# Modulation in four lots of columns, most of each summed on VectorE and used at once by gate and up tile

## The chip, the cores and the metric

The kernel runs on one core of a Trainium2 chip: TensorE (PE) for matmuls, VectorE (DVE), ScalarE (ACT) and GpSimd (POOL) for work on elements, SyncE (SP), whose queue issues nearly all transfers, SBUF as working memory and eight banks of PSUM, into which TensorE writes. The metric is device time in microseconds, the median of the runs.

## The reference

Two stacks of layers over 512 tokens of width 1024, in float32. What matters here is the very start: the conditioning vector c gives shift, scale and gate of each sub-layer, and the first sub-layer is a gated feed-forward.

```python
c_act = jax.nn.silu(c)
mod = c_act @ ada_w[i] + ada_b[i]
sh1, sc1, g1, sh2, sc2, g2, sh3, sc3, g3 = jnp.split(mod, N_MOD, axis=-1)
h = modulate(rms_norm(x, ln_ffn1[i]), sh1, sc1)
x = x + 0.5 * g1[:, None, :] * swiglu(h, ffn1_wg[i], ffn1_wu[i], ffn1_wd[i])
```

The first matmul of the feed-forward needs sh1 and sc1, 2048 columns of ada_w[0], which are 8 MB of weights: 1024 x 2048 values of 4 bytes.

## The kernel before

Activations lie transposed, 8 blocks (kb) of 128 features by 512 tokens. Every weight tile has 8 blocks of 256 columns, 1 MB. SP loads it into a slot of w_raw, ScalarE casts it in two halves to w_hi_t (w_hi counts them), GpSimd subtracts that from the raw values to give w_lo_t (w_lo), and each product is three matmuls: high x high, high x low and low x high, 48 matmuls of 512 columns a tile (16 blocks and column halves by 3). The activations are split the same way, into h_hi and h_lo. Tiles alternate between two slots; in a feed-forward a gate tile (slot 0, banks 0 and 1) and an up tile (slot 1, banks 2 and 3) make a pair. After a pair ScalarE takes Silu of the gate banks, VectorE multiplies (v_done), ScalarE copies the high part (a_hi_s), VectorE makes the low part (a_lo_s). The next pair's gate waits for v_done, since it writes the banks again.

Engines have a written order of instructions each, and meet by semaphores. At the start (SP lines 699 to 720) c, the identity, the first 256 columns of ada_w, six of eight blocks of shift columns in four quarters (first_a), x, and the 1024 scale columns in four quarters (first_b) are loaded, then the first gate and up tile. TensorE sums the first 256 columns itself (L2094, 16 matmuls of one column), VectorE the other 1792 as rows (L1477 and L1480: accumulator + row block of weights x c), of which TensorE adds up the partitions by matmuls with ones (first_sums, L2068). Then VectorE makes gain and mod of all 16 column blocks (ada_fin) and the normed input block by block: start_scaled (x * gain * root, L1525), ScalarE adds the shift into h_hi (L1101), start_low gives h_lo (L1531). The root of the mean square is in bank 6. start_units on TensorE (L2081 to L2085) follows with the gate tile alone; the up tile and all others run in unit (L1916 to L1921): all high products first, then the eight with w_lo.

While the feed-forward runs, VectorE also sums the next modulation columns: ada_step (L1427, L1430), one row block of 1024 columns each, out of a ring of four buffers that SP fills once mod_ok says that the first modulation is done; each eight steps end with a transpose and a reduce. Five steps go to each of the first four pairs, ahead of that pair's products on VectorE's queue. Between the first and the second pair stand two small matmuls for the attention bias (L2127, L2128).

## Time and profile before

| | us |
|---|---|
| median of 3 runs | 2597.61 (2597.54 to 2598.28) |
| the profiled execution | 2597.89 |
| its span | 2596.1 |
| TensorE busy in the span | 2555.4 |

The profiled execution is the one the rows below come from; its time is the span and what lies around it. Times in rows are counted from the start of the span. Busy times of an engine overlap those of the others, and a matmul's record is longer than the distance to the next, since matmuls are pipelined: the chain of waits shows the distance.

### The profile page before, as it was taken

What the parts mean: (1) busy time and instruction counts of PE and PEld (TensorE: products, weight loads), DVE (VectorE), ACT (ScalarE), POOL (GpSimd) and SP (SyncE); (2) the same over time, 40 slices, a digit from 0 to 9 for tenths busy, and PEclk for the clock granted to TensorE, in tenths of its full rate; (3) what the DMA queues carried; (4) which work ended last, traced back from release to release, by engine and by line L of the source; (5) the groups of instructions that cost most, each with busy time, mean ns of one, the idle gap of its engine ahead of it and who ended that gap; (6) DMA issues with size and microseconds to landing.
All of it is one profiled execution on the core that took longest, in us unless ns stands there. A gap on an engine that the chain in (4) does not pass through costs nothing.

```text
span 2596.1 us, 30205 instructions
## 1 busy us (share of the span) xinstructions
PE 2555.4 (98%) x12530; PEld 2122.6 (82%) x12530; DVE 1090.7 (42%) x1543; ACT 910.8 (35%) x1395; POOL 998.4 (38%) x404
## 2 busy tenths in 40 slices
PE   6999999999999999999999999999999999999999
PEld 5888888776888888888888988888888888888887
DVE  6626254545532325854445255211146555512213
ACT  3222234565422223422224334222244444423324
POOL 2445444221444444444444434444440000444442
PEclk8999999999999999999999999999999999999999
DMA  8645344111333343545452323323222221333231
GB/s 295 208 165 190 120 155 129 60 56 49 114 130 130 130 138 106 203 154 186 138 189 87 115 81 130 114 98 126 93 86 83 76 70 49 98 97 97 96 96 69
DMA packets 249214, 312.13 MB, mean 120 GB/s; under 512 B 7356, under 2 KB 227149, under 8 KB 248950
## 3 DMA queue, kind: packets, MB, share of 16 engines
q1 hardware_dynamic: 246762, 308.88, 35.3%
q8 instruction: 99, 1.62, 0.3%
q10 hardware_dynamic: 2316, 1.33, 0.2%
q14 instruction: 37, 0.30, 0.0%
HBM read 308.07 MB, written 4.74 MB: 120 GB/s over the span
## 4 chain that ended last, share of the span: by engine, by line
PE 94%; DVE 3%; issue 1%; ACT 1%; POOL 0%; DVEq 0%; ACTq 0%
PE bank L1921 21%; PE bank L1916 21%; PE bank L1917 21%; PE bank L1933 5%; PE bank L1934 5%; PE bank L1938 5%; PE bank L1899 2%; PE bank L1900 1%; PE bank L1901 1%; PE bank L1948 1%; PE bank L1949 1%; PE bank L1950 1%; PE bank L1841 1%; PE bank L1755 1%; PE bank L1775 1%
## 5 line engine op out<-in xcount | busy, mean ns | idle before, releaser
L809 POOL TENSOR_TENSOR w_lo_t<-w_raw,w_hi_t 128x1024 fp32r<-128x1024 f32 (+1 forms) x400 | 998.2, 2515 | 1572.7 <-ACT w_hi_t L981 1572.3
L981 ACT CAST w_hi_t<-w_raw 128x1024 fp32r<-128x1024 f32 (+1 forms) x432 | 424.9, 1032 | 692.9 <-PE bank L1921 576.3
L1916 PE MATMUL bank<-h_hi,w_hi_t 128*128 128x512 f32 x1648 | 642.1, 390 | 0.0
L1917 PE MATMUL bank<-h_lo,w_hi_t 128*128 128x512 f32 x1648 | 641.2, 389 | 0.0
L1921 PE MATMUL bank<-h_hi,w_lo_t 128*128 128x512 f32 x1648 | 415.2, 391 | 0.0
L1916 PEld LDWEIGHTS bank<-h_hi,w_hi_t 128*128 128x128 f32 x1648 | 309.3, 188 | 64.3 <-issue 0.5
L1917 PEld LDWEIGHTS bank<-h_lo,w_hi_t 128*128 128x128 f32 x1648 | 309.4, 188 | 64.1 <-issue 0.2
L1921 PEld LDWEIGHTS bank<-h_hi,w_lo_t 128*128 128x128 f32 x1648 | 309.3, 188 | 64.0
L1430 DVE SCALAR_TENSOR_TENSOR scr<-scr,cact 128x1024 f32<-128x1024 f32 x112 | 251.1, 2242 | 75.4 <-DMA scr<-in_ada_w 67.7
L1916 PE MATMUL bank<-act_hi,w_hi_t 128*128 128x512 f32 x720 | 280.3, 389 | 0.3 <-DVE x L1636 0.2
L1917 PE MATMUL bank<-act_lo,w_hi_t 128*128 128x512 f32 x720 | 280.1, 389 | 0.0
L1611 DVE TENSOR_TENSOR bank<-hidden,bank 128x512 f32<-128x512 f32 x88 | 61.1, 694 | 439.4 <-ACT hidden L1142 439.4
L1636 DVE SCALAR_TENSOR_TENSOR x<-bank,half,x 128x512 f32<-128x512 f32 x88 | 66.1, 751 | 338.1 <-PE bank L1921 260.9
L1142 ACT ACTIVATE hidden<-bank 128x512 f32<-128x512 f32 x88 | 52.7, 599 | 370.4 <-PE bank L1921 370.4
L1921 PE MATMUL bank<-act_hi,w_lo_t 128*128 128x512 f32 x720 | 178.7, 389 | 0.1
L1916 PEld LDWEIGHTS bank<-act_hi,w_hi_t 128*128 128x128 f32 x720 | 135.1, 188 | 29.1 <-DVE x L1636 0.6
L1921 PEld LDWEIGHTS bank<-act_hi,w_lo_t 128*128 128x128 f32 x720 | 135.1, 188 | 28.5 <-POOL w_lo_t L809 0.5
L1917 PEld LDWEIGHTS bank<-act_lo,w_hi_t 128*128 128x128 f32 x720 | 135.2, 188 | 28.1
L1933 PE MATMUL bank<-act_hi,w_hi_t 128*128 128x512 f32 x320 | 128.1, 400 | 0.1
L1934 PE MATMUL bank<-act_lo,w_hi_t 128*128 128x512 f32 x320 | 124.7, 390 | 0.0
L1933 PE MATMUL bank<-h_hi,w_hi_t 128*128 128x512 f32 x288 | 121.1, 421 | 0.0
L1938 PE MATMUL bank<-act_hi,w_lo_t 128*128 128x512 f32 x320 | 114.3, 390 | 0.0
(275 smaller groups left out, 3337.0 us busy)
## 6 DMA issues: line engine op xcount, KB each, us to landing
scr<-in_ada_w SPq DMA_DIRECT2D x128, 512.0 KB, 6.6
w_raw<-in_ffn_wg SPq DMA_DIRECT2D x44, 1024.0 KB, 5.2
w_raw<-in_ffn_wu SPq DMA_DIRECT2D x44, 1024.0 KB, 5.2
w_raw<-in_ffn_wd SPq DMA_DIRECT2D x32, 1024.0 KB, 4.8
w_raw<-in_mlp_w SPq DMA_DIRECT2D x32, 1024.0 KB, 5.2
w_raw<-in_hgrn_w_in SPq DMA_DIRECT2D x16, 1024.0 KB, 5.4
w_raw<-in_ffn_wd SPq DMA_DIRECT2D x16, 768.0 KB, 4.3
w_raw<-in_attn_w_qkv SPq DMA_DIRECT2D x12, 1024.0 KB, 5.1
```

The source lines that it names most:

```text
L809: nc.gpsimd.tensor_tensor(w_lo_t[:, t % 2, k], w_raw[:, t % 2, k], w_hi_t[:, t % 2, k].bitcast(F32), ALU.subtract).then_inc(w_lo, 1)
L981: act.copy(w_hi_t[:, slot, k], w_raw[:, slot, k]).then_inc(w_hi, 1)
L1142: act.activation(blk(hidden, 4 + (2 * i + b) % 4), ps[b][:], ACT.Silu).then_inc(act1, 1)
L1430: dve.scalar_tensor_tensor(acc, src, cact[:, kb:kb + 1], acc, ALU.mult, ALU.add).then_inc(ada_ch, 1)
L1611: dve.tensor_tensor(ps[2 + b][:], blk(hidden, 4 + (2 * i + b) % 4), ps[2 + b][:], ALU.mult).then_inc(v_done, 1)
L1636: ins_ = dve.scalar_tensor_tensor(xb, acc[:], gate_col(op, nb), xb, ALU.mult, ALU.add)
L1916: pe.matmul(dst, w, blk(m_hi, kb), start=kb == 0, stop=False)
L1917: pe.matmul(dst, w, blk(m_lo, kb), start=False, stop=False)
L1921: last = pe.matmul(dst, w_lo_t[:, slot, kb, b * P:(b + 1) * P], blk(m_hi, kb), start=False, stop=kb == kbs - 1)
L1933: pe.matmul(dst, w, blk(m_hi, kb), start=kb == 0, stop=False)
L1934: pe.matmul(dst, w, blk(m_lo, kb), start=False, stop=False)
L1938: last = pe.matmul(dst, w_lo_t[:, slot, kb, b * P:(b + 1) * P], blk(m_hi, kb), start=False, stop=kb == kbs - 1)
```

## The change

The 16 column blocks of the first modulation are made in four lots. A lot is two blocks of shift and two of scale columns, so that it gives all that kb 2p and 2p + 1 of the normed input need. Three of the four column blocks are summed on VectorE (rows, 384 columns), the fourth on TensorE (sums); TensorE then adds VectorE's partitions into the same bank. As soon as a lot's modulation is there, VectorE and ScalarE make its two blocks of h, and TensorE uses them with the gate tile and the up tile, which now share start_units and hold banks 0 to 3 at once. SP loads x first, then lot 0, the first gate tile, lot 1, the first up tile, lots 2 and 3; then the small vectors. A few biases come in early by two loads of their own. The root of the mean square moves from bank 6 to SBUF (rstd), since bank 6 now takes scaled blocks. The first five ada_step go behind the first pair's products, and their loads behind the second pair's weights. The transposes of the small vectors go behind the first pair's matmuls, and the second pair's gate waits for Silu alone instead of the product.

The core of the diff:

```diff
+        PART_AT = (0, 4096, 8192, 0)
+        part_w = [scr[:, c:c + 4096].rearrange("p (k n) -> p k n", k=KB) for c in PART_AT]
+        part_acc = [hidden[:, c:c + 3 * P] for c in (2304, 2688, 3072, 3456)]
+        part_sum = [ps[7 if p % 2 else 5] for p in range(4)]
...
-        H_BANK = (ps[4], ps[5], ps[2])
+        H_BANK = (ps[4], ps[6])
...
+            def part(p, q):
+
+                for half in range(2):
+                    c0 = half * D + 2 * p * P
+                    sp.dma_start(part_w[p][:, 2 * q:2 * q + 2, half * TW:half * TW + TW],
+                                 first_w[:, 2 * q:2 * q + 2, c0:c0 + TW]).then_inc(part_in[p][q], 16)
...
+            for p in range(2):
+                for q in range(4):
+                    part(p, q)
+                weight(p, p, tile_src(("ffn1_wg", "ffn1_wu")[p], 0, 0, KB)[:, :, 0:TW], skip_wait=True)
...
+            for q in range(4):
+                part(2, q)
+            small_rows(0, 4)
+            sp.wait_ge(part_mm, 1)
+            for q in range(4):
+                part(3, q)
+            small_rows(4, len(rows))
...
+                        ahead = 0 if first and i == 0 else RING - 1
+                        for s in steps[:ahead]:
                             ada_step(s)
                         if i + 1 < op.nb // 2:
                             pair(i + 1)
-                        for s in steps[RING - 1:]:
+                        for s in steps[ahead:]:
...
-                        act.activation(ps[6][:], ps[6][:], ACT.Exp, scale=-0.5).then_inc(root_ok, 2)
+                        act.activation(rstd[:], rstd[:], ACT.Exp, scale=-0.5).then_inc(root_ok, 2)
...
+                            if kb == 4:
+                                conv(1, 1)
...
+                        early = op.t0 == i == 0
+                        if not early:
+                            conv_at(0, nxt, i, 2)
...
+            def rows(p, q):
+
+                acc = part_acc[p]
+                dve.wait_ge(part_in[p][q], 16 * 2)
+                for kb in (2 * q, 2 * q + 1):
+                    src, c = part_w[p][:, kb, 0:3 * P], cact[:, kb:kb + 1]
+                    if kb == 0:
+                        ins_ = dve.tensor_scalar(acc, src, c, None, ALU.mult)
+                    else:
+                        dve.wait_ge(part_dv, KB * p + kb)
+                        ins_ = dve.scalar_tensor_tensor(acc, src, c, acc, ALU.mult, ALU.add)
+                    ins_.then_inc(part_dv, 1)
+
+            def part_mod(p):
+
+                bank, a, b = part_sum[p], slice(2 * p, 2 * p + 2), slice(DB + 2 * p, DB + 2 * p + 2)
+                dve.wait_ge(part_mm, p + 1)
+                link(dve.tensor_tensor(bank[:, 16:18], bank[:, b], vec[:, b], ALU.add))
+                dve.scalar_tensor_tensor(gain[:, 0, 0, a], bank[:, 16:18], 1.0, vec[:, V_LN + 2 * p:V_LN + 2 * p + 2],
+                                         ALU.add, ALU.mult)
+                link(dve.tensor_tensor(mod[:, 0, a], bank[:, a], vec[:, a], ALU.add))
...
+            for p in range(4):
+                part_mod(p)
+                start_scaled(2 * p)
+                start_scaled(2 * p + 1)
+                if p in (0, 2):
+                    rows(p + 1, 0)
+                start_low(2 * p)
+                start_low(2 * p + 1)
+                for q in range(0 if p == 1 else 1, 4 if p < 3 else 0):
+                    rows(p + 1, q)
+            dve.memset(small[:, 5:6], 0.0).then_inc(mod_ok, 1)
+            dve.wait_ge(mod_ok, 1)
+            dve.wait_ge(init_a, 2)
+            link(dve.tensor_tensor(neg_lam, small[:, 7:8], small[:, 6:7], ALU.subtract))
+            link(dve.tensor_scalar(neg_lam, neg_lam, -LAMBDA_INIT, None, ALU.add))
+            dve.wait_ge(init_p, 10)
...
+                        late = op.t0 == i == 0
+                        for s in ada_steps(op, i) if op.ada and not late else ():
                             ada_step(s)
...
+                        for s in ada_steps(op, i) if late else ():
+                            ada_step(s)
...
+            def start_tile(op, s, kb):
+
+                t = op.t0 + s
+                for b in range(2):
+                    if b == 0:
+                        pe.wait_ge(w_hi, 2 * t + kb // 4 + 1)
+                    pe.matmul(ps[2 * s + b][:], w_hi_t[:, s, kb, b * P:(b + 1) * P], blk(h_hi, kb), start=kb == 0, stop=False)
+                w_half(t, kb // 4)
+                for b in range(2):
+                    pe.matmul(ps[2 * s + b][:], w_lo_t[:, s, kb, b * P:(b + 1) * P], blk(h_hi, kb), start=False, stop=False)
+                pe.wait_ge(h_lo_s, 2 * kb + 2)
+                for b in range(2):
+                    mm = pe.matmul(ps[2 * s + b][:], w_hi_t[:, s, kb, b * P:(b + 1) * P], blk(h_lo, kb),
+                                   start=False, stop=kb == KB - 1)
+                    if kb == KB - 1:
+                        mm.then_inc(blk_mm, 1)
+
+            def part_sums(p):
+
+                for q in range(4):
+                    sums(p, q, (3,))
+                pe.wait_ge(part_dv, KB * (p + 1))
+                for i in range(3):
+                    col = DB * (i // 2) + 2 * p + i % 2
+                    mm = pe.matmul(part_sum[p][:, col:col + 1], part_acc[p][:, i * P:(i + 1) * P],
+                                   ones[:, 0:1], start=False, stop=True, skip_group_check=True)
+                mm.then_inc(part_mm, 1)
+
+            def start_blocks(op, s, *blocks):
+
+                for kb in blocks:
+                    pe.wait_ge(h_hi_s, 2 * kb + 2)
+                    start_tile(op, s, kb)
+
             def start_units(op):
 
-                w_half(op.t0, 0)
-                for kb in range(KB):
-                    if kb == 4:
-                        w_half(op.t0, 1)
-                    pe.wait_ge(h_hi_s, 2 * kb + 2)
-                    for b in range(2):
-                        cols = slice(b * P, (b + 1) * P)
-                        pe.matmul(ps[b][:], w_hi_t[:, 0, kb, cols], blk(h_hi, kb), start=kb == 0, stop=False)
-                        pe.matmul(ps[b][:], w_lo_t[:, 0, kb, cols], blk(h_hi, kb), start=False, stop=False)
-                    pe.wait_ge(h_lo_s, 2 * kb + 2)
-                    for b in range(2):
-                        mm = pe.matmul(ps[b][:], w_hi_t[:, 0, kb, b * P:(b + 1) * P], blk(h_lo, kb),
-                                       start=False, stop=kb == KB - 1)
-                        if kb == KB - 1:
-                            mm.then_inc(blk_mm, 1)
+                start_blocks(op, 0, 0, 1)
+                part_sums(1)
+                start_blocks(op, 0, 2, 3)
+                start_blocks(op, 1, 0, 1, 2)
+                part_sums(2)
+                start_blocks(op, 1, 3)
+                start_blocks(op, 0, 4, 5)
+                start_blocks(op, 1, 4)
+                part_sums(3)
+                start_blocks(op, 1, 5)
+                start_blocks(op, 0, 6, 7)
+                start_blocks(op, 1, 6, 7)
+                pe.wait_ge(cst_in, 16 * 18)
+                for grp, (c0, n) in enumerate(((0, 72), (128, 72), (V_LN, V_COLS - V_LN))):
+                    mm = pe.transpose(ps[4][:, c0:c0 + n], vrow[0:n, grp, :], ident[0:n, 0:n])
+                mm.then_inc(init_p, 1)
...
+                                if s == 0 and op.t0 == 0 and i == 1:
+                                    pe.wait_ge(act1, b + 1)
+                                elif s == 0:
```

VectorE, from the first modulation to the first pair's products. Before (rows of a lot are `hidden<-scr,cact,hidden`, scaled blocks `bank<-x,gain,...`, low parts `h_lo<-...`):

```order
L1480 SCALAR_TENSOR_TENSOR hidden<-scr,cact,hidden 128x1024 [waits ada_dv_ok,ada_b_in3]
L1514 MEMSET small 128x1 [waits x_init]
L1515 MEMSET small 128x1
L1455 TENSOR_TENSOR bank<-bank,vec 128x8 [waits ada_mm]
L1456 SCALAR_TENSOR_TENSOR gain<-bank,vec 128x8 [waits chain]
L1457 TENSOR_TENSOR mod<-bank,vec 128x16
L1464 MEMSET small 128x1 [waits chain]
L1525 SCALAR_TENSOR_TENSOR bank<-x,gain,bank 128x512 [waits root_ok,mod_ok]
L1525 SCALAR_TENSOR_TENSOR bank<-x,gain,bank 128x512
L1531 SCALAR_TENSOR_TENSOR h_lo<-bank,mod,h_hi 128x512 [waits h_hi_s]
L1525 SCALAR_TENSOR_TENSOR bank<-x,gain,bank 128x512
```

VectorE now, the same place, at lot 0 and the start of lot 1:

```order
L1491 TENSOR_TENSOR bank<-bank,vec 128x2 [waits part_mm]
L1492 SCALAR_TENSOR_TENSOR gain<-bank,vec 128x2 [waits chain]
L1494 TENSOR_TENSOR mod<-bank,vec 128x2
L1532 SCALAR_TENSOR_TENSOR bank<-x,gain,rstd 128x512 [waits root_ok,chain]
L1532 SCALAR_TENSOR_TENSOR bank<-x,gain,rstd 128x512
L1481 TENSOR_SCALAR hidden<-scr,cact 128x384 [waits part_in10]
L1484 SCALAR_TENSOR_TENSOR hidden<-scr,cact,hidden 128x384 [waits part_dv]
L1538 SCALAR_TENSOR_TENSOR h_lo<-bank,mod,h_hi 128x512 [waits h_hi_s] x2
L1484 SCALAR_TENSOR_TENSOR hidden<-scr,cact,hidden 128x384 [waits part_dv,part_in11]
```

The rows of the next lot now stand between one lot's blocks and the next lot's modulation, and rstd takes the place of the bank as an operand of the scaled block.

VectorE at the products of the first pair (`bank<-hidden,bank`), before:

```order
L1427 TENSOR_SCALAR scr<-scr,cact 128x1024 [waits ada_in0,chain]
L1430 SCALAR_TENSOR_TENSOR scr<-scr,cact 128x1024 [waits ada_ch,ada_in1]
L1430 SCALAR_TENSOR_TENSOR scr<-scr,cact 128x1024 [waits ada_ch,ada_in2]
L1430 SCALAR_TENSOR_TENSOR scr<-scr,cact 128x1024 [waits ada_ch,ada_in3]
L1430 SCALAR_TENSOR_TENSOR scr<-scr,cact 128x1024 [waits ada_ch,ada_in0]
L1611 TENSOR_TENSOR bank<-hidden,bank 128x512 [waits blk_mm,act1] x2
L1615 TENSOR_TENSOR act_lo<-bank,act_hi 128x512 [waits a_hi_s] x2
L1603 TENSOR_SCALAR hidden<-bank 8x512 [waits bias_sb]
```

And now:

```order
L1621 TENSOR_TENSOR bank<-hidden,bank 128x512 [waits blk_mm,act1,chain]
L1621 TENSOR_TENSOR bank<-hidden,bank 128x512 [waits blk_mm,act1]
L1625 TENSOR_TENSOR act_lo<-bank,act_hi 128x512 [waits a_hi_s] x2
L1431 TENSOR_SCALAR scr<-scr,cact 128x1024 [waits ada_in0]
L1434 SCALAR_TENSOR_TENSOR scr<-scr,cact 128x1024 [waits ada_ch,ada_in1]
L1434 SCALAR_TENSOR_TENSOR scr<-scr,cact 128x1024 [waits ada_ch,ada_in2]
L1434 SCALAR_TENSOR_TENSOR scr<-scr,cact 128x1024 [waits ada_ch,ada_in3]
L1434 SCALAR_TENSOR_TENSOR scr<-scr,cact 128x1024 [waits ada_ch,ada_in0]
L1612 TENSOR_SCALAR hidden<-bank 8x512 [waits bias_sb]
```

The five steps have moved behind the products and low parts, so that ten steps now stand between the products of the first pair and those of the second.

## Rows read from the trace of the kernel before

**Rows 1.** The page, part 1: busy us, share of the span, instructions.

```profile
PE 2555.4 (98%) x12530; PEld 2122.6 (82%) x12530; DVE 1090.7 (42%) x1543; ACT 910.8 (35%) x1395; POOL 998.4 (38%) x404
```

**Rows 2.** Windows: us, busy by engine (instructions), PEclk, DMA share, GB/s.

```profile
20.00:25.00 5.00, 1.37 (x11) 0.89 (x9) 4.55 (x5) 4.29 (x10) 0.00 (x0) 1.00 1.03 407
...
30.00:38.00 8.00, 0.70 (x3) 0.41 (x3) 5.98 (x8) 0.69 (x2) 0.00 (x0) 0.50 1.06 356
...
50.00:69.00 19.00, 19.00 (x85) 15.46 (x84) 15.75 (x21) 6.33 (x9) 8.24 (x4) 1.00 0.75 262
69.00:92.15 23.15, 23.15 (x101) 18.48 (x102) 16.60 (x13) 6.18 (x8) 12.03 (x4) 1.00 0.53 191
```

**Rows 3.** Chain of waits, 42 to 92 us: start, us, what.

```profile
42.87 0.77 DVE bank L1525
43.72 0.70 ACT h_hi L1101
44.55 0.76 PE bank L2081
45.31 0.43 PE bank L2082
...
67.19 1.81 PE bank L1921 x8
69.00 0.95 PE bank L2127 x2
70.17 0.43 PE bank L1916
...
90.34 1.81 PE bank L1921 x8
```

**Rows 4.** Timeline, 0 to 42 us: start, us, engine, line, tile, count [idle before].

```profile
2.70 0.47 SPq L703 DMA_DIRECT2D scr<-in_x  x1
...
16.01 1.06 ACT L1065 ACTIVATE x<-scr 128x1024 f32<-128x1024 f32 x1 [11.21 <-DMA scr<-in_x]
...
20.31 4.01 ACT L1061 COPY x<-bank 128x512 f32<-128x512 f32 x8
...
29.45 0.66 ACT L1094 ACTIVATE bank<-bank,small 128x512 f32<-128x512 f32 x1 [5.12 <-PE bank L2108]
...
33.85 0.70 PE L2112 MATMUL bank<-ident,hidden 72*128 72x72 f32 x3 [4.45 <-DMA hidden<-in_sgu_ln_b]
...
38.57 3.58 PE L2068 MATMUL bank<-ones,hidden 128*128 128x1 f32 x16 [4.02 <-DVE hidden L1480]
38.78 1.99 ACT L981 CAST w_hi_t<-w_raw 128x1024 fp32r<-128x1024 f32 x2 [8.00 <-DMA w_raw<-in_ffn_wg]
```

**Rows 5.** Groups by shape, 0 to 70 us: count, busy us, mean ns, idle before.

```profile
L1480 DVE SCALAR_TENSOR_TENSOR hidden<-scr,cact,hidden 128x1024 f32<-128x1024 f32 x7 | 9.0, 1285 | 2.5 <-DMA scr<-in_ada_w 1.4 <-DVE vec L1509 0.6
...
L1480 DVE SCALAR_TENSOR_TENSOR hidden<-scr,cact,hidden 128x768 f32<-128x768 f32 x7 | 7.1, 1019 | 7.4 <-DMA scr<-in_ada_w 6.7
...
L1531 DVE SCALAR_TENSOR_TENSOR h_lo<-bank,mod,h_hi 128x512 fp32r<-128x512 f32 x8 | 6.0, 746 | 0.5 <-ACT h_hi L1101 0.5
```

**Rows 6.** Timeline, 47 to 66 us, of VectorE and of GpSimd.

```profile
47.71 2.38 POOL L809 TENSOR_TENSOR w_lo_t<-w_raw,w_hi_t 128x1024 fp32r<-128x1024 f32 x1 [3.15 <-ACT w_hi_t L981]
47.81 0.74 DVE L1525 SCALAR_TENSOR_TENSOR bank<-x,gain,bank 128x512 f32<-128x512 f32 x1
...
56.56 9.55 DVE L1430 SCALAR_TENSOR_TENSOR scr<-scr,cact 128x1024 f32<-128x1024 f32 x4
...
59.29 5.74 POOL L809 TENSOR_TENSOR w_lo_t<-w_raw,w_hi_t 128x1024 fp32r<-128x1024 f32 x2 [6.54 <-ACT w_hi_t L981]
```

**Rows 7.** Timeline of VectorE, 71 to 83 us.

```profile
71.63 0.67 DVE L1603 TENSOR_SCALAR hidden<-bank 8x512 f32<-8x512 f32 x1
72.23 0.27 DVE L1604 TENSOR_SCALAR hidden<-bank 8x128 f32<-8x128 f32 x1
72.43 7.94 DVE L1430 SCALAR_TENSOR_TENSOR scr<-scr,cact 128x1024 f32<-128x1024 f32 x3
80.41 1.25 DVE L1437 STREAM_TRANSPOSE scr<-scr 128x1024 f32<-128x1024 f32 x1
81.69 1.22 DVE L1438 TENSOR_REDUCE ada_r<-scr 128x32 f32<-128x1024 f32 x1
```

More of the change, by code:

```diff
@@ L480, in build_program @@
         ada_in = [sem(f"ada_in{i}") for i in range(4)]
-        ada_pe_in = sem("ada_pe_in")
         c_in = sem("c_in")
         x_init = sem("x_init")
-        ada_a_in = [sem(f"ada_a_in{i}") for i in range(4)]
-        ada_b_in = [sem(f"ada_b_in{i}") for i in range(4)]
+        part_in = [[sem(f"part_in{p}{q}") for q in range(4)] for p in range(4)]
+        part_dv = sem("part_dv")
+        part_mm = sem("part_mm")
+        early_in = sem("early_in")
+        early_mm = sem("early_mm")
+        early_ok = sem("early_ok")
         pat_in = sem("pat_in")
-        ada_dv_ok = sem("ada_dv_ok")
-        ada_pe_ok = sem("ada_pe_ok")
         small_in = sem("small_in")
@@ L703, in _ @@
             sp.dma_start(x_nat, ins["x"][0].rearrange("(t p) d -> p t d", p=P)).then_inc(xin, 16)
-            for q in range(1, 4):
-                first_a(q)
-            first_b(0)
-            sp.wait_ge(ada_dv_ok, 3)
-            first_b(1)
-            small_rows(0, 9)
-            sp.wait_ge(ada_dv_ok, 6)
-            first_b(2)
-            small_rows(9, len(rows))
+            for p in range(2):
+                for q in range(4):
+                    part(p, q)
+                weight(p, p, tile_src(("ffn1_wg", "ffn1_wu")[p], 0, 0, KB)[:, :, 0:TW], skip_wait=True)
@@ L1451, in ada_fin @@
             def ada_fin(layer, m0, m1, count, derive):
-                dve.wait_ge(ada_mm, count)
-                if count == 1:
-                    scale = ps[5][:, 16:16 + DB]
-                    link(dve.tensor_tensor(scale, ps[5][:, DB:2 * DB], vec[:, V_ADA[0] + DB:V_ADA[0] + 2 * DB], ALU.add))
-                    dve.scalar_tensor_tensor(gain[:, 0, 0, :], scale, 1.0, vec[:, V_LN:V_LN + DB], ALU.add, ALU.mult)
-                link(dve.tensor_tensor(mod[:, layer, m0:m1], ps[5 if count == 1 else 7][:, m0:m1],
+                dve.wait_ge(ada_mm, count - 1)
+                link(dve.tensor_tensor(mod[:, layer, m0:m1], ps[7][:, m0:m1],
                                        vec[:, V_ADA[layer] + m0:V_ADA[layer] + m1], ALU.add))
@@ L1547, in _, with start_scaled, start_low @@
             dve.tensor_scalar(qk_gain[:, 0:1], qk_gain[:, 0:1], -Q_SCALE, None, ALU.mult)
+            dve.wait_ge(x_init, DB)
+            dve.memset(stat[:, 0:1], 0.0).then_inc(x_upd, DB)
+            dve.memset(small[:, 5:6], 0.0).then_inc(v_done, 2)
+            op = ops[0]
+            def start_scaled(kb):
+                if kb == 0:
+                    dve.wait_ge(root_ok, 2)
+                if kb >= 2:
+                    dve.wait_ge(h_lo_s, 2 * kb - 2)
+                dve.scalar_tensor_tensor(H_BANK[kb % 2][:], blk(x, kb), gain_col(op, kb), rstd[:], ALU.mult, ALU.mult)\
+                   .then_inc(h_t, 2)
+            def start_low(kb):
+                dve.wait_ge(h_hi_s, 2 * kb + 2)
+                dve.scalar_tensor_tensor(blk(h_lo, kb), H_BANK[kb % 2][:], shift_col(op, kb), blk(h_hi, kb).bitcast(F32),
+                                         ALU.add, ALU.subtract).then_inc(h_lo_s, 2)
+            for p in range(4):
[14 more added lines that the diff above has]
+            dve.wait_ge(init_p, 10)
+            for c0, c1 in ((0, 72), (128, 200), (V_LN, V_COLS)):
+                ins_ = dve.tensor_copy(vec[:, c0:c1], ps[4][:, c0:c1])
+            link(ins_)
             dve.tensor_scalar(sub_gain, vec[:, V_SUB:V_SUB + 1], 1.0 - LAMBDA_INIT, None, ALU.mult)
@@ L2090, in _ @@
-            pe.wait_ge(init_a, 1)
-            pe.wait_ge(ada_pe_in, 16)
-            for b in range(2):
-                for kb in range(KB):
-                    mm = pe.matmul(ps[5][:, b:b + 1], ada_pe[:, kb, b * P:(b + 1) * P],
-                                   cact[:, kb:kb + 1], start=kb == 0, stop=kb == KB - 1)
-            mm.then_inc(ada_pe_ok, 1)
+            pe.wait_ge(early_in, 16 * 2)
+            pe.transpose(ps[4][:, 0:3 * DB], early_rows, ident[0:3 * DB, 0:3 * DB]).then_inc(early_mm, 1)
@@ new lines, in sums @@
+            def sums(p, q, blocks):
+                pe.wait_ge(part_in[p][q], 16 * 2)
+                for kb in (2 * q, 2 * q + 1):
+                    for i in blocks:
+                        col = DB * (i // 2) + 2 * p + i % 2
+                        mm = pe.matmul(part_sum[p][:, col:col + 1], part_w[p][:, kb, i * P:(i + 1) * P],
+                                       cact[:, kb:kb + 1], start=kb == 0 and i == blocks[0], stop=kb == KB - 1,
+                                       skip_group_check=True)
+                return mm
@@ L2104, in _ @@
             pe.wait_ge(init_d, 1)
[L2105 to L2106 removed]
             pe.wait_ge(ssq_done, 9)
             pe.matmul(ps[6][:], ones[:], ssq[:], start=True, stop=True).then_inc(ssum_mm, 2)
[L2109 to L2115 removed]
+            part_sums(0)
+            pe.wait_ge(x_init, DB)
             norm, npre = None, 0
@@ L2139, in _ @@
                                     start_units(op)
[L2140 removed]
+                                    break
                                 w_half(t, 0)
```

117 lines of the change are left out of this document (25 added, 92 removed).

## The prediction

> **What bounds the kernel now.** I read the page first: TensorE is busy 98% of the span [rows 1], so a change pays only where TensorE idles or runs slowly. The stretches [rows 2] show where: from 30 to 38 us it is busy 0.70 of 8 us, and from 50 us on it is busy without a gap, the first pair (gate and up tile) to 69, the second to 92.15. The chain of waits [rows 3] gives the order of the start: first scaled block on VectorE at 42.87, first high part on ScalarE at 43.72, first product at 44.55. One matmul then costs 0.43 us, and 0.226 later (eight in 1.81): TensorE starts at the half clock, 0.50 in [rows 2], since it had idled. The pair ends at T = 69.00, the second at 92.15 [rows 3]. Behind T everything is the same program apart from what is named below, so the answer is how T moves, and whether the second pair still runs without a gap.
>
> **The opening, step by step.** At most it could gain the 24.4 us from 44.55 to 69.00 less what must follow the last lot: 24 matmuls, 5.4 us. But the lots form a chain VectorE – TensorE – VectorE – ScalarE – TensorE, which I walk through.
>
> *Start.* x is issued at 2.70 us and has landed at 16.01 [rows 4]; 1.84 MB of modulation weights in front of it go. At the 0.38 MB/us between the two rates of [rows 2] (0.407 and 0.356) that is 4.8 us, so x lands at about 10.8. The squares and copies on ScalarE take 8.3 us (16.01 to 24.32) [rows 4]: 19.1. Then Ln and Exp, 0.6 each after the 0.66 of [rows 4], and two casts, 1.99: 22.2. The first lot's rows are ready by then, its sums at 20.8.
>
> *Costs that repeat.* A row of the old sum takes 1.019 us at 768 columns and 1.285 at 1024 [rows 5], so 1.04 us per 1000 columns and 0.62 at 384 columns; with the 0.1 between two dependent rows 0.72, eight 5.7. The chain of sums to first scaled block is 0.7 (38.57 + 3.58 to 42.87 [rows 3, 4]), mostly the small modulation operations, 0.5. A scaled block takes 0.74 [rows 6], a low part 0.746 [rows 5], a high part 0.70 [rows 3]. Eight matmuls of one column took 3.58 us at half clock [rows 4], 0.45 each; the three behind VectorE's rows then cost 0.75 to 1.3.
>
> *VectorE against GpSimd.* GpSimd's w_lo subtraction takes 2.38 us alone. While it ran, a scaled block whose second operand was in a bank took its usual 0.74 (47.81). But of four modulation rows with both operands in SBUF, starting at 56.56, the two that met two subtractions made the four last 9.55 instead of 5.5, and the subtractions 5.74 instead of 4.8 [rows 6]: they take turns, one whole instruction at a time. The new rows are of that kind, and the new scaled block becomes so, since rstd moves from bank 6 to SBUF. The Trainium skill, page "SBUF — State Buffer", section "SBUF: two separate sides", states this as a lock that a VectorE instruction with two SBUF inputs and a GpSimd instruction hold in turn for the whole instruction; the rows at 56.56 agree, and no run here shows it for a scaled block. By it that block pays 2.4 us too; were the block free, the rows behind it would pay instead, and the sum stays.
>
> *The four lots.*
> Lot 1: from 20.8, modulation 0.5, scaled 0.75 (22.0), a subtraction 2.4, scaled 0.75, a subtraction 2.4 (27.5), two rows, two low parts (30.2), six rows (34.3). TensorE: gate blocks 0 and 1 wait for the low parts, then 2.6 us at half clock and 2 to 3.5 of column sums: the three last end at 35.8.
> Lot 2: modulation and two scaled 2.0, low parts to 39.4; eight rows 5.3 and the two subtractions of the second tile, 4.7, cast only behind the fourth high part: 49.4. TensorE's 30 matmuls (6.8 at full, 12.8 at half clock, from 37.9) end by then at mixed clock. Sums: 50.6.
> Lot 3: modulation, two scaled, two rows, two low parts 4.7 (55.3), six rows 4.2 (59.4), sums 1.2: 60.6.
> End: modulation 0.5, scaled 0.75, high part 0.7 and hand-overs 0.2: 62.8; 24 matmuls at 0.226: T = 68.2, against 69.0. **Term 1: -0.8 us.** Bounds: without any of the four subtractions in the way 9.5 less on VectorE, of which TensorE, then the later one in lots 1 and 2, gives back 3: T = 61.8 (-7.2). With lot 2's 30 matmuls and the end at half clock, T = 72 (+3).
> Transfers don't decide this: all four lots, x and two weight tiles are 12.6 MB, done by about 38 us at the same rates, while VectorE reads lot 3 after 52.
>
> **Behind the first pair.** The 72-row transposes, 0.70 us [rows 4], hidden before 44 us, now stand behind the pair: **term 2: +0.6** (the overlap with the last matmul taken off; bounds 0.3 and 0.7).
> VectorE's queue is the real worry. Before, five modulation rows of the next columns (0 to 4) ran under the first pair, until 66.1 [rows 6]. Now mod_ok comes only at the end of lot 3, and the rows stand behind the pair's products, ahead of rows 5 to 9 and of the second pair's products; for these the third pair's gate waits (v_done). Counted from T: transposes, vec copies and small operations 1.6, which the first pair's products now wait for; products and low parts 2.8: 4.4. Row 0, 0.75 (5.2); a subtraction of tile 3, 2.4; row 1, 1.28; the other 2.4 (11.2); rows 2 to 4, 1.38 each (15.3); bias copies 0.95 [rows 7] (16.3); rows 5 to 7, 4.1 (20.4); transpose and reduce 2.5 [rows 7] (22.9); the two subtractions of tile 4, 4.7, the first of which starts 1.2 before the reduce has ended, around rows 8 and 9, 2.1 (28.5); product 0.7: 29.2. TensorE arrives there at T + 0.6 + 1.15 for the bias products + 22.0 (70.17 to 92.15 [rows 3]) = T + 23.75. **Term 3: +5.4 us** of idle TensorE. Before, the same stretch had VectorE busy 16.6 of 23.15 us [rows 2], three rows there taking 7.94 [rows 7]; five rows more are 6.4 without any wait, which with the 6.5 free would just about fit: lower bound 0. Upper bound 6.5, if one more subtraction falls among them.
> While it idles the clock falls, as it stood at 0.50 after the idle stretch from 30 us [rows 2]. The start of the third pair then runs some 9 matmuls at 0.43 instead of 0.226: **term 4: +1.8** (0 if it stays up; 12 matmuls at half clock were what the start before needed, 2.5).
>
> **Sum.** -0.8 + 0.6 + 5.4 + 1.8 = +7.0 us. The profiled execution took 2597.89 us around a span of 2596.1; 2604.9 on its scale, and 2604.6 on that of the median, 2597.61, which lies 0.28 lower. Edits that I take at nothing: the early biases (two small loads, a transpose and two copies under the wait for x; without that cover under 1 us), the order of casts and Silu (ScalarE is busy a third of 50 to 69 us [rows 2]), the eight column sums of a lot (under VectorE's rows; uncovered they cost 2 to 3.5 us a lot, and in lot 3 they end only 0.5 behind the rows).
>
> **Rivals.** (a) *Faster:* VectorE's rows hardly meet the subtractions. For: GpSimd works only 9.5 us in the opening. Against: every one of the four falls into VectorE's work, in lots 1 and 2. Then T = 61.8, and VectorE is done with the second pair in time: -7.2 + 0.6 + 0.4 = -6.2, 2591.4. It decides once the rows of lots 1 and 2 all take 0.6 us.
> (b) *No change:* the opening comes out even and VectorE's backlog dissolves, because tile 4's subtraction falls behind rows 8 and 9 (4.7 less) and row 0 to 4 find a free port: stall under 1, no clock fall: -0.8 + 0.6 + 0.5, 2597.9. It hangs on when tile 4's weights land, behind rows 5 to 7 in SP's queue.
> (c) *Slower still:* the clock stays low through the lots. TensorE now works in bursts between idle stretches; before, it fell to 0.50 in the idle stretch behind the transposes. Between the sums of lots 1 and 3 stand 54 matmuls, each 0.2 dearer at half clock, 10.8 us, of which waits for VectorE hide 5 to 7: T = 72 to 74, with terms 2 to 4 2608.5 to 2610.5. The Trainium skill, page "TensorE: Matmul & The Clock Gate", section "HAM oscillation — how this bites in real kernels", warns of just such bursts with waits between; the 0.50 behind the idle stretch agrees.
>
> **Chances.** The forecast 0.45; (a) 0.18; (b) 0.25; (c) 0.12. The bound of 0.2%, 5.2 us, is about what a measurement of this kernel can tell from no change. Faster 0.20 (a, and 0.02 of forecasts with a lucky opening), same 0.25, slower 0.55. Own range of the forecast: terms 1 and 3 at -2 and 4 to +2 and 6.5, 2602 to 2609. To leave out no more than 2 in 10 the range takes in (a) and most of (c): 2591.5 to 2611.
>
> **What would show it.** Right: column sums of lots 1 to 3 ending near 36, 51 and 61 us; rows of 0.6 us, and of about 3 where a subtraction runs; scaled blocks above 2 us beside w_lo; first matmul near 23, the pair's end near 68; TensorE waiting 4 to 6 us for VectorE's product before the third pair, the clock at 0.50 behind it. Wrong: the pair's end at 62 or earlier (a), no wait before the third pair (b), an end of the pair beyond 71 with matmuls at 0.43 (c). If x lands after 13, every number of the opening shifts by what it is late.

## The result and the profile after

| | before | after |
|---|---|---|
| median, us (five runs each) | 2597.61 | 2610.78 |
| lowest to highest | 2596.60 to 2598.55 | 2606.40 to 2612.29 |
| the profiled execution, span | 2597.89, 2596.1 | 2606.40, 2604.6 |

The ratio is 1.0048, with an interval of 1.0037 to 1.0059: slower by 13.2 us in the median. The profiled execution is the quickest of its five, and its span is 8.5 us longer than that of before. So two things have to be explained: the 8.5, and the other 4 to 5 us of the median.

The chain of waits after, behind the first pair (start, us, what), with the rows that answer to the end of [rows 3]:

```profile
90.66 1.81 PE bank L1933 x8
92.47 6.53 issue
99.00 0.77 PE bank L1928
99.77 0.43 PE bank L1929
...
101.47 0.43 PE bank L1929
101.90 0.37 PE bank L1928
102.27 0.23 PE bank L1929
```

The second pair ends at 92.47, where it ended at 92.15 before: up to here the change has cost 0.32. Then TensorE stands still for 6.53 us, and its next matmuls take 0.43 instead of 0.23 until 102.27. Together that is the 8.5, less some 0.1: 0.3 + 6.5 + 1.5 to 1.6.

The timeline of that stretch after the change: VectorE's rows, and between them what SP issues and what ScalarE and GpSimd do next (start, us, engine, line, tile, count, idle before):

```profile
74.09 9.35 DVE L1434 SCALAR_TENSOR_TENSOR scr<-scr,cact 128x1024 f32<-128x1024 f32 x4
...
82.52 0.43 SPq L657 DMA_DIRECT2D w_raw<-in_ffn_wg  x1
83.00 1.14 SPq L657 DMA_DIRECT2D w_raw<-in_ffn_wu  x1
84.16 2.65 DVE L1434 SCALAR_TENSOR_TENSOR scr<-scr,cact 128x1024 f32<-128x1024 f32 x2
84.62 12.69 SPq L666 DMA_DIRECT2D scr<-in_ada_w  x5
87.57 1.28 DVE L1434 SCALAR_TENSOR_TENSOR scr<-scr,cact 128x1024 f32<-128x1024 f32 x1 [0.76 <-DMA scr<-in_ada_w]
...
90.17 1.22 DVE L1442 TENSOR_REDUCE ada_r<-scr 128x32 f32<-128x1024 f32 x1
90.57 2.00 ACT L980 CAST w_hi_t<-w_raw 128x1024 fp32r<-128x1024 f32 x2 [16.07 <-DMA w_raw<-in_ffn_wg]
91.70 4.66 POOL L808 TENSOR_TENSOR w_lo_t<-w_raw,w_hi_t 128x1024 fp32r<-128x1024 f32 x2 [12.12 <-ACT w_hi_t L980]
94.80 2.11 DVE L1431 TENSOR_SCALAR scr<-scr,cact 128x1024 f32<-128x1024 f32 x1 [3.41 <-DMA scr<-in_ada_w]
97.01 1.28 DVE L1434 SCALAR_TENSOR_TENSOR scr<-scr,cact 128x1024 f32<-128x1024 f32 x1
98.21 1.28 DVE L1621 TENSOR_TENSOR bank<-hidden,bank 128x512 f32<-128x512 f32 x2
```

The product that TensorE waits for is the row at 98.21. Ahead of it VectorE is late with its own work until 91.4: four of the five steps that ran under the first pair before (56.56 in [rows 6]) now run from 74.09 on. Then it idles 3.41 us for the data of step 8 (steps are counted from 0), which stand in SP's queue behind the third pair's weights (82.52, 83.00), and these behind step 7.

The opening, from the timeline of the same execution:

```profile
23.05 1.42 DVE L1532 SCALAR_TENSOR_TENSOR bank<-x,gain,rstd 128x512 f32<-128x512 f32 x2
23.33 1.99 ACT L980 CAST w_hi_t<-w_raw 128x1024 fp32r<-128x1024 f32 x2 [1.85 <-DMA w_raw<-in_ffn_wg]
...
24.46 4.79 POOL L808 TENSOR_TENSOR w_lo_t<-w_raw,w_hi_t 128x1024 fp32r<-128x1024 f32 x2 [24.02 <-ACT w_hi_t L980]
24.85 2.18 DVE L1481 TENSOR_SCALAR hidden<-scr,cact 128x384 f32<-128x384 f32 x1 [0.37 <-DMA scr<-in_ada_w]
...
26.26 1.19 PE L2096 MATMUL bank<-h_hi,w_hi_t 128*128 128x512 f32 x2 [3.77 <-ACT h_hi L1104]
27.06 2.60 DVE L1484 SCALAR_TENSOR_TENSOR hidden<-scr,cact,hidden 128x384 f32<-128x384 f32 x1
...
33.90 1.84 PE L2085 MATMUL bank<-cact,scr 128*128 128x1 f32 x16
35.60 0.81 PE L2114 MATMUL bank<-ones,hidden 128*128 128x1 f32 x6
...
40.38 8.68 DVE L1484 SCALAR_TENSOR_TENSOR hidden<-scr,cact,hidden 128x384 f32<-128x384 f32 x7
```

Its windows (us, busy by engine, PEclk, DMA share, GB/s), to be read beside [rows 2]:

```profile
25.00:30.00 5.00, 2.04 (x4) 1.12 (x4) 4.96 (x3) 1.58 (x4) 4.25 (x2) 0.50 1.10 348
30.00:38.00 8.00, 6.03 (x30) 5.24 (x30) 6.03 (x13) 0.18 (x1) 0.00 (x0) 0.71 1.11 347
38.00:44.50 6.50, 5.94 (x15) 4.69 (x16) 6.14 (x6) 3.05 (x4) 4.32 (x2) 0.53 1.05 321
```

Two rows of lot 1 take 2.18 and 2.60 us beside a subtraction, where 0.41 and 0.62 is usual, and lot 2's last seven take 8.68 beside two subtractions instead of some 4.7. TensorE works from 26.3 on, 18 us earlier than before, but waits for VectorE, and between 25 and 44 us it is mostly at 0.50. So the 18 us are gone by the pair's end, at 69.08 by the chain (69.00 before). TensorE spends the 42.8 us from 26.3 to 69.1 so: 4.6 on waits, 7.3 on the column sums of lots 1 to 3, 21.7 on the 96 matmuls at 0.226 each; the 9.3 that are left are what the half clock costs (2.7 of the 24.4 us before).

### The profile page after: what moved, and what is told of

It reads as the page before. It is cut to its first block, busy times and chain, and to the rows that moved or that the text cites. A ratio compares the mean times of both kernels' runs of the same rounds, so it can differ in the third digit from the quotient of the medians.

```text
span 2604.6 us, 30328 instructions
## 1 busy us (share of the span) xinstructions
PE 2560.7 (98%) x12559; PEld 2126.0 (82%) x12559; DVE 1101.1 (42%) x1570; ACT 910.1 (35%) x1395; POOL 995.9 (38%) x404
## 3 DMA queue, kind: packets, MB, share of 16 engines
q8 instruction: 99, 1.62, 0.3%
## 4 chain that ended last, share of the span: by engine, by line
PE 93%; DVE 3%; issue 1%; ACT 1%; POOL 0%; DVEq 0%; ACTq 0%
PE bank L1933 21%; PE bank L1928 20%; PE bank L1929 20%; PE bank L1945 5%; PE bank L1946 5%; PE bank L1950 5%; PE bank L1911 2%; PE bank L1912 1%; PE bank L1913 1%; PE bank L1960 1%; PE bank L1961 1%; PE bank L1962 1%; PE bank L1853 1%; PE bank L1767 1%; PE bank L1787 1%
```

## The experiments

My theory: the loss is the backlog behind the first pair (the wait and the half clock in its wake), and the opening comes out even. Rivals: the opening's clock; late data rather than VectorE's work. In the table the end of the first pair is the start of the next small matmul in TensorE's timeline (68.93 before, 68.92 after), and the wait is that before the third pair. Both come from one profiled execution; medians are over all runs. "Steps" are the 20 modulation steps (ada_step) that run under the four pairs of the first gate and up tiles. Ahead of the fourth pair TensorE does not wait before, after or in e1; in e2, e6, e10 and e11 it waits 0.94 or 0.95 us there, in e8 1.89.

| run | first pair ends | wait | median | ratio to before, interval |
|---|---|---|---|---|
| e1_repeat | 71.50 | 6.41 | 2609.46 | 1.0046, 1.0033 to 1.0060 |
| e2_spread | 72.02 | none | 2602.69 | 1.0020, 1.0011 to 1.0028 |
| e3_rows_in_bank | 67.32 | 6.38 | 2604.65 | 1.0029, 1.0017 to 1.0040 |
| e4_old_opening_late | 68.54 | 4.87 | 2605.14 | 1.0030, 1.0019 to 1.0042 |
| e5_tiles_first | 69.12 | 4.72 | 2606.77 | 1.0038, 1.0025 to 1.0052 |
| e6_bank_spread | 69.87 | none | 2597.19 | 1.0003, 0.9994 to 1.0011 |
| e7_all_rows | 70.35 | 5.77 | 2607.57 | 1.0043, 1.0030 to 1.0056 |
| e8_all_rows_spread | 70.01 | none | 2601.52 | 1.0018, 1.0009 to 1.0027 |
| e9_warm | 68.83 | 6.92 | 2609.19 | 1.0046, 1.0034 to 1.0059 |
| e10_mixed | 65.55 | none | 2597.64 | 1.0003, 0.9993 to 1.0012 |
| e11_mixed_warm | 63.20 | none | 2595.31 | 0.9993, 0.9984 to 1.0001 |
| e12_deal_0668 | 66.66 | none | 2596.48 | 0.9995, 0.9986 to 1.0004 |

### The changed kernel once more (e1_repeat)

No edit. 

> The changed kernel again, unchanged, for a second profile: its five runs reach from 2606.4 to 2612.3, those of before only from 2596.6 to 2598.6. Theory A (the spread is the clock's: TensorE's bursts in the lots catch it at 0.50 or at 1.00): a run slower than 2606.4 shows more time at 0.50 up to the first pair's end, which then lies at 70 to 72 and not at 69.1; the wait before the third pair stays 6 to 7. Theory B (the spread is the data's): the first pair ends at 69 again and the wait before the third pair is 8 us or more in a slower run.

Its five runs lie at 2609.2 to 2609.7, and the profiled one took 2609.68. That agrees with theory A. Windows of this second profile:

```profile
30.00:38.00 8.00, 6.67 (x24) 5.89 (x24) 5.55 (x9) 0.00 (x0) 0.20 (x1) 0.50 1.10 347
38.00:44.50 6.50, 4.35 (x15) 3.69 (x16) 4.47 (x9) 3.23 (x4) 1.13 (x1) 0.50 1.07 325
```

TensorE's column sums of lot 1, from its timeline:

```profile
34.91 3.41 PE L2085 MATMUL bank<-cact,scr 128*128 128x1 f32 x16
38.18 1.42 PE L2114 MATMUL bank<-ones,hidden 128*128 128x1 f32 x6
```

The clock stays at 0.50 through 30 to 38 us, where the first profile has 0.71. The 22 one-column passes (eleven matmuls, two passes each) take 4.83 us instead of 2.65, and lot 2's modulation, which waits for them, starts at 39.6 instead of 36.5. The pair ends 2.6 us later, the wait is about the same (6.41), and the span is 3.1 longer. A smaller part of this came earlier: lot 0's last rows waited longer for their data and ended 0.6 us later.

### Without the backlog (e2_spread)

```diff
     pairs = op.nb // 2
+    if op.t0 == 0:
+        at = (0, 0, 6, 13, 20)
+        return range(at[i], at[i + 1])
```

> The changed kernel, but the 20 modulation steps that run under the first up and gate columns are dealt 0, 6, 7, 7 to the four pairs instead of 5, 5, 5, 5, so that none stands between the first pair's products and the six of the second pair. Theory (the loss is the backlog behind the first pair): the wait before the third pair falls from 6.5 to under 1 and the clock stays at 1.00 there; 8 us come back: 2598 to 2600.5 where the profiled run had 2606.4, and 2601 to 2603 if the median stays 4 above the best run. Rival (the opening itself loses, by its clock): 2606 or more remain. Rival (steps run under later pairs now delay those): 2603 to 2606.

The wait before the third pair is gone, and 6.8 us come back against e1_repeat's median. 5.5 us stay: in its profile the first pair ends at 72.02, 3.1 us later than before, and 0.94 us are a new wait ahead of the fourth pair. There the first scaled blocks started beside a subtraction, and they paid this time, not the rows of lot 1 (VectorE, timeline; 1.42 in the rows above):

```profile
26.35 4.44 DVE L1535 SCALAR_TENSOR_TENSOR bank<-x,gain,rstd 128x512 f32<-128x512 f32 x2
```

So the backlog is the larger part of the loss and not all of it. Theory and both rivals each hold in part.

### Rows that do not meet GpSimd (e3_rows_in_bank)

```diff
+        part_bank = [ps[5 if p % 2 else 7][:, P:4 * P] for p in range(4)]
...
-                acc = part_acc[p]
...
+                    acc = part_bank[p] if p else part_acc[p]
+                    dst = part_acc[p] if kb == KB - 1 else acc
...
-                        ins_ = dve.scalar_tensor_tensor(acc, src, c, acc, ALU.mult, ALU.add)
+                        ins_ = dve.scalar_tensor_tensor(dst, src, c, acc, ALU.mult, ALU.add)
```

> The changed kernel, but the row sums of lots 1 to 3 are accumulated in a PSUM bank (the last row of a lot is written to SBUF), so that a row has one operand in SBUF instead of two. Theory (rows and GpSimd's subtractions take turns because both operands lie in SBUF): no row of lots 1 and 2 takes above 0.8 us, the sums of lot 1 end 4 us earlier, those of lot 2 up to 8 us earlier. If VectorE sets the opening throughout, the first pair then ends at 61 to 63 instead of 69.1; if TensorE at the half clock sets it as soon as VectorE is quicker, at 65 to 67. The wait before the third pair stays at 5 to 7, so 2599 to 2601 or 2603 to 2605 against 2606.4. Rival (turns are taken whatever the operands): nothing changes, 69.

VectorE and GpSimd side by side, lots 1 and 2:

```profile
24.42 4.81 POOL L809 TENSOR_TENSOR w_lo_t<-w_raw,w_hi_t 128x1024 fp32r<-128x1024 f32 x2 [23.98 <-ACT w_hi_t L981]
24.80 0.62 DVE L1483 TENSOR_SCALAR bank<-scr,cact 128x384 f32<-128x384 f32 x1
25.46 0.62 DVE L1486 SCALAR_TENSOR_TENSOR bank<-scr,cact,bank 128x384 f32<-128x384 f32 x1
...
38.13 4.71 POOL L809 TENSOR_TENSOR w_lo_t<-w_raw,w_hi_t 128x1024 fp32r<-128x1024 f32 x2 [8.91 <-ACT w_hi_t L981]
38.54 4.12 DVE L1486 SCALAR_TENSOR_TENSOR bank<-scr,cact,bank 128x384 f32<-128x384 f32 x6
```

With the accumulator in a bank every row takes 0.6 to 0.7 beside a subtraction, and the subtractions take their usual 2.4. That shows that the rows' turns hang on the place of their operands. But the first pair ends at 67.32, 1.6 us earlier and not 7: from here TensorE is the later engine, and VectorE waits 3 and 5.5 us for the sums of lots 1 and 2. The median falls by 4.8 us.

### The backlog alone (e4_old_opening_late)

The kernel before, with this on VectorE and nothing else:

```diff
-                        for s in ada_steps(op, i) if op.ada else ():
+                        late = op.t0 == i == 0
+                        for s in ada_steps(op, i) if op.ada and not late else ():
                             ada_step(s)
...
+                        for s in ada_steps(op, i) if late else ():
+                            ada_step(s)
```

> The kernel before, with one part of the change alone: on VectorE the first five modulation steps go behind the first pair's products. Theory (the backlog makes the loss, whatever the opening): the first pair ends at 69.0 as before, TensorE waits 4 to 6 us before the third pair and starts it at clock 0.50: +5 to +8 us, 2603 to 2606. Rival (the opening of the change is needed for the wait, since its small work and transposes come first): a wait under 2 and a time below 2600.

The chain of waits:

```profile
91.76 4.87 issue
96.63 0.47 PE bank L1919
97.10 0.42 PE bank L1920
```

8.0 us slower than before, with the old opening: the place of the five steps alone is enough for a wait and a half clock of this kind. The wait is 4.87 here and 6.4 to 6.5 in the changed kernel.

### Data or work (e5_tiles_first)

```diff
-                        ahead = 0 if first and i == 0 else RING - 1
+                        ahead = 0 if first and i < 2 else RING - 1
```

> The changed kernel, but in SP's queue the third pair's weights stand ahead of modulation steps 5 to 9 instead of between step 7 and step 8. In the changed kernel those weights are issued only at 82.5 us, their cast waits until 90.6, and step 8's row waits 3.4 us for its data. Theory A (half of the wait is late data): without that wait VectorE reaches the second pair's products some 3 us earlier, the wait before the third pair is 2.5 to 4 and not 6.5, 2602.5 to 2604 against the 2606.4 of the first profile, or 2606 to 2608 against a median near 2610. Theory B (VectorE's own work fills the time: GpSimd's two subtractions of tile 4 only move forward among rows 5 to 9): the wait stays at 5 to 6.5 and the time within 1.5.

The wait falls to 4.72, between the two theories, and the time by 2.7 us against e1_repeat. The weights' split now runs from 83 us, and with it the turns move (VectorE and GpSimd):

```profile
82.97 5.28 POOL L808 TENSOR_TENSOR w_lo_t<-w_raw,w_hi_t 128x1024 fp32r<-128x1024 f32 x2 [3.18 <-ACT w_hi_t L980]
...
86.39 5.73 DVE L1434 SCALAR_TENSOR_TENSOR scr<-scr,cact 128x1024 f32<-128x1024 f32 x3 [1.95 <-DMA scr<-in_ada_w]
...
94.56 0.74 DVE L1431 TENSOR_SCALAR scr<-scr,cact 128x1024 f32<-128x1024 f32 x1
```

Step 8 no longer waits, but step 5 does, 1.95 us, and three rows take 5.73 instead of 4.0. In either order a step's data stand behind the weights and are late. Of 6.5 us some 2 are the order of the loads.

### Both repairs (e6_bank_spread)

The edits of e3 and e2. 

> Both repairs together: row sums in a PSUM bank as in e3_rows_in_bank, steps dealt 0, 6, 7, 7 as in e2_spread. Theory (the two losses are independent): the 5 to 6 us of the opening's repair and the 7 to 8 of the backlog's add up: the first pair ends at 67 to 70, the second runs on into the third without a wait, 2596 to 2599, that is as the kernel before within 0.1%. Rival (with the opening quicker the backlog's repair has less to give, or the steps delay later pairs): 2600 or more.

2597.19: no difference from before can be measured. The sum of the two single gains against e1_repeat, 6.8 + 4.8, is 11.6, and 12.3 were measured, which fits two independent losses. The opening in four lots with both repairs is worth nothing in the median.

The profiled run, 2601.15, is among the slowest of its eleven, and it was not free of turns: the rows no longer meet a subtraction, but the first two scaled blocks, whose x and rstd lie in SBUF, did.

```profile
24.08 3.51 DVE L1537 SCALAR_TENSOR_TENSOR bank<-x,gain,rstd 128x512 f32<-128x512 f32 x2
```

GpSimd's first subtraction starts at 24.4 to 25.1 in every profile of an opening in lots. Where the second of the two blocks starts before it (the changed kernel's two profiles, e3, e5, e9, e10, e11), the two take 1.42; where it does not (e2, e6, e7, e8, e12), they take 3.5 to 5.5. In the kernel before, with the root in a bank, a block took 0.74 beside a subtraction (47.81 in [rows 6]). No run here kept the root in a bank, so what that would be worth stays open.

### All column blocks on VectorE (e7_all_rows, e8_all_rows_spread)

On top of e3, and of e6:

```diff
-                    src, c = part_w[p][:, kb, 0:3 * P], cact[:, kb:kb + 1]
+                    src, c = part_w[p][:, kb, :], cact[:, kb:kb + 1]
...
-                for q in range(4):
-                    sums(p, q, (3,))
                 pe.wait_ge(part_dv, KB * (p + 1))
-                for i in range(3):
+                for i in range(4):
```

> e3_rows_in_bank, but all four column blocks of a lot are summed on VectorE (512 columns a row instead of 384), and TensorE's sixteen one-column matmuls a lot are gone: it only adds up the partitions. Theory (TensorE's one-column sums, 2.6 us a lot at either clock, and the fall to 0.50 that follows them in each lot, set the opening once rows no longer meet subtractions): VectorE has room for rows of 0.75; 1.8 us a lot go away in lots 1 to 3 and the dips behind lots 2 and 3 get shorter or vanish; the first pair ends at 60 to 63 against 67.5, and the time falls by 4 to 7 against e3_rows_in_bank: 2598 to 2601. Rival (VectorE decides again, with 32 longer rows): 66 to 68, 2603 to 2605.

> e7_all_rows with the steps dealt 0, 6, 7, 7. Theory: as e7_all_rows less the wait of 6.4 and the half clock behind it: 2590 to 2594, faster than both kernels. Rival (the opening does not gain by it): 2596 to 2599 as e6_bank_spread.

2607.57 and 2601.52: 2.9 and 4.3 slower than e3 and e6. The theory fell, and its premise, 2.6 us a lot at either clock, does not hold at 0.50 (4.83 in e1). Lot 1's last row ends at 37.6 instead of 31.4 in e3, and TensorE now idles for it (1.62 us ahead of its sums). Of these 6.2 us only 1 is the longer rows, eight at 0.75 instead of 0.62. Another 4.1 is a meeting: lot 0's sums ended 1.3 us later, and the scaled blocks ran beside both subtractions (e7, 1.42 in e3):

```profile
24.62 5.49 DVE L1534 SCALAR_TENSOR_TENSOR bank<-x,gain,rstd 128x512 f32<-128x512 f32 x2
```

In lot 3, where no subtraction runs, TensorE idles 1.94 us ahead of its sums, so there VectorE, with the longer rows, is the later engine. What rows of 512 columns cost without that meeting is not shown.

### Matmuls into the waits (e9_warm)

```diff
+            def warm(bank, n):
+
+                for _ in range(n):
+                    pe.matmul(bank[:], ones[:], ssq[:], start=True, stop=True)
...
+                warm(ps[7], 2)
                 start_blocks(op, 0, 0, 1)
                 part_sums(1)
+                warm(ps[5], 1)
                 start_blocks(op, 0, 2, 3)
```

> The changed kernel plus three matmuls of 512 columns whose result nobody reads: two while TensorE waits for the first high part (3.8 us idle), one while it waits for the third (2.2 us idle). Theory (TensorE's clock in lots 1 and 2 makes the difference between runs and 2 to 3 us of the opening): 0.50 in less of the stretch from 23 to 44 us, the first pair ends at 66 to 69, and five runs lie within 2.5 us of each other: 2605 to 2607 against medians of 2609.5 to 2610.8. Rival (the one-column sums alone let the clock fall, whatever fills the waits): 0.50 as before from 23.6 on, and 2609 to 2612.

A miss: 2609.19, and the runs lie 4.4 us apart. The window from 26 to 30 us has 0.89 instead of 0.50, but from 38 to 42 it is 0.50 again, and TensorE waits for VectorE's low parts there anyway. The profile shows a second place where executions differ: behind the wait of 6.92 us the half clock lasts until 105.5, 6.3 us, while in both profiles of the changed kernel it lasted about 3. The program from there on is the same, so term 4 may be 1.5 or 3 us by the run; no two profiles of one kernel show it.

### Column sums between the blocks (e10_mixed, e11_mixed_warm)

On top of e6; e11 adds the matmuls of e9.

```diff
+                for p, blocks in ((1, ((0, 0), (0, 1))), (2, ((0, 2), (0, 3), (1, 0), (1, 1), (1, 2))),
+                                  (3, ((1, 3), (0, 4), (0, 5), (1, 4)))):
+                    for n, (s, kb) in enumerate(blocks):
+                        start_blocks(op, s, kb)
+                        for q in range(2 * n, 2 * n + 2) if p == 1 else range(n, min(n + 1, 4)):
+                            sums(p, q, (3,))
+                    part_sums(p)
```

> e6_bank_spread, but the sixteen one-column matmuls of a lot no longer stand in one block: four of them follow each block of gate or up tile (eight in lot 1). Theory (the block of one-column work lets the clock fall): no fall to 0.50 behind the sums of lots 2 and 3, and TensorE works on lot 1's sums while it waits for low parts; the first pair ends at 64 to 66 instead of 69.9: 2592 to 2595. Rival (the clock falls anyway, or VectorE's rows set the sums' end): 67 to 70, 2596 to 2598.

> e10_mixed plus the three matmuls of e9_warm. Theory: the clock stays at 1.00 from 26 us on; the first pair ends at 62 to 65 and the runs lie within 2.5 us: 2590 to 2594. Rival: as e10_mixed, or up to 2 us slower for the added matmuls.

Two windows of e6_bank_spread:

```profile
50.00:55.00 5.00, 5.00 (x24) 4.19 (x24) 3.17 (x8) 1.35 (x2) 0.00 (x0) 0.66 0.49 159
60.00:65.00 5.00, 5.00 (x22) 3.76 (x23) 3.31 (x10) 2.25 (x3) 0.00 (x0) 0.68 0.00 0
```

The same two of e10_mixed:

```profile
50.00:55.00 5.00, 4.17 (x22) 3.22 (x23) 4.79 (x9) 1.27 (x2) 0.00 (x0) 1.00 0.89 288
60.00:65.00 5.00, 5.00 (x22) 4.13 (x23) 1.74 (x5) 4.05 (x6) 0.10 (x1) 1.00 0.47 152
```

Where sixteen of the 22 one-column passes no longer stand in a block, the clock does not fall behind them: 1.00 instead of 0.66 and 0.68, although TensorE is less busy. In the profiled executions the first pair ends at 65.55 and, with the added matmuls, at 63.20. The 4.3 us between e6 and e10 are not all the clock's: 2.1 more went to e6's scaled blocks beside a subtraction, and e3, whose blocks were clear of it, ended at 67.32. The medians follow only in part: 2597.64, no better than e6's 2597.19, and 2595.31, each over 11 runs that lie 6 and 9 us apart. e11's is the lowest, 2.1 us below that of before, and its interval still touches 1: no version here is shown to beat the kernel before. The granted clock over the whole execution goes with it: e11's runs at 0.999 took 2592.0 and 2592.6, the one at 2601.2 has 0.995.

### The steps dealt again (e12_deal_0668)

e11 with (0, 0, 6, 12, 20). 

> e11_mixed_warm with the steps dealt 0, 6, 6, 8 instead of 0, 6, 7, 7. In its trace the last wait that the kernel before does not have is 0.94 us in front of the fourth pair, for the third pair's product, with the clock at 0.50 behind it. Theory (the same backlog, smaller): with one step less ahead of that product the wait and the half clock behind it go, 1.5 to 2.5 us: a median of 2592.8 to 2594, faster than before by about 0.15%. Rival (the eighth step delays the fourth pair's products instead, and the next tiles wait): 2595 to 2597.

2596.48: nothing gained. The wait of 0.94 ahead of the fourth pair is gone, but there was no half clock behind it to gain, as I had supposed: in e11's trace the clock is 1.00 there. And another wait has come at the first tile of the next stage (chain of waits):

```profile
124.77 7.38 DMA w_raw<-in_ffn_wd
132.22 1.06 ACT w_hi_t L984
...
133.35 2.38 POOL w_lo_t L812
...
135.77 0.50 PE bank L1950
```

TensorE waits 0.75 us for that tile's low parts, whose weights were loaded behind the eight steps. Its first pair ended at 66.66 and e11's at 63.20, with the same instructions up to there. Two things differ: from 34 to 38 us the clock is 0.50 here and 0.69 there, and the first scaled blocks met a subtraction here (3.52) and not there (1.42).

## Why the prediction was right, and where not

**Term 1, the opening (-0.8).** Measured +0.1 in the first profile, +2.6 in the second. Column sums ended at 36.4, 50.6 and 60.1 (36, 51 and 61 were said), and x was used from 11.1 on. The cause named holds, with three corrections. The first matmul came at 26.3 and not near 23: I took transfers to decide nothing, but in the first 20 us they moved 0.23 MB/us and not 0.38, lot 0's last rows waited for data until 20.3, and the gate tile lands behind lot 0, so that its cast starts at 23.3. For that reason the scaled blocks were done before the subtractions and the rows paid, as the text allowed ("the rows behind it would pay instead"); in e2 the blocks paid. That the sums still ended where I had said is partly luck: lot 0's sums were 1.7 us late (22.5), and the turns in lot 1 cost 3.7 us and not 4.8. The end was mis-sized: I priced the last 24 matmuls at the full clock, 5.4 us, and they took 6.8 (62.29 to 69.08), the clock being at 0.50 until 64.5. And the case at 0.50, "T = 72 (+3)", which I took for a bound, is near what the slower profiles show (71.50 in e1, 72.02 in e2).

**Term 2, the transposes (+0.6).** The second pair's first matmul comes 1.41 us behind the first pair's end instead of 1.17: 0.24, a little under the lower bound.

**Term 3, the wait (+5.4).** 6.53 and 6.41, and 6.92 in e9, at or just over the upper bound of 6.5; right in place and in kind, as e4 and e2 show. Its last part was mis-sized: I put 4.7 us of tile 4's subtractions around rows 8 and 9, assuming their data to be there. In fact SP's queue holds both the tile and those data back (3.41 of idle), and only one subtraction meets a row.

**Term 4, the clock (+1.8).** About 1.5 in both profiles of the changed kernel, about 3 in e9.

**The sum.** +7.0 was said, and the profiled execution shows +8.5. The median shows +13.2, outside the forecast's own range and only 0.2 us inside the upper end of the whole range, which reached that far for the sake of rival (c): that it was not missed is partly luck. What is missing is what rival (c) described: lots at the half clock, T at 72, 2608.5 to 2610.5. I gave it as the other case at 0.12; by their times nine of the ten runs of the changed kernel may be of this kind (2608.7 and more), but only one of them is traced (e1), and at 2609.68 it lies below the median of the first five. What the rest of that median is stays open; term 4 at 3 us instead of 1.5, as in e9, would be enough, but no run of this kernel shows it. That the lots' clock differs from run to run is shown (e1); what decides it in a run is not, and filling two waits did not settle it (e9). Whether the first scaled blocks meet a subtraction also differs from run to run (e11 against e12, with the same instructions up to there). Rival (a) supposed that with rows clear of the subtractions T would be 61.8, of 9.5 us less on VectorE 3 given back by TensorE. e3 made them clear, and T was 67.3: TensorE, partly at the half clock, gives back most of it, not 3. Rival (b) fell with the first trace.

## What to carry to other kernels

Work that is moved off a startup path lands on a queue that was full already: count, from the new place on, everything that is queued ahead of the next result that another engine waits for, the loads in their queue as well. Cutting a startup into a chain of lots starts TensorE early but in short bursts, and then the clock that it is granted decides how much of the early start survives; price such lots at both levels. Before two engines are given work to do side by side, look where the operands lie: an accumulator in PSUM instead of SBUF took away the turns between VectorE and GpSimd, and the root, moved from PSUM to SBUF, brought such turns to the scaled blocks.
